# Retention chunks of a hybrid decoder trunk: the cross term is moved beside the scores on TensorE's other row half, and two transposes a chunk take the place of three

## The reference

```python
def retention(q, k, v):
    # chunks of C = 128 tokens; decay, xi, zeta, chunk_decay are fixed numbers of the head
    scores = einsum(qc, kc) * decay
    o_inner = einsum(scores, vc)
    kz = kc * zeta
    def step(R, inp):
        q_n, kz_n, v_n = inp
        o = q_n @ R                       # what earlier chunks add
        R = R * chunk_decay + kz_n.T @ v_n
        return R, o
    o_cross = scan(step, R0, ...) * xi
    return o_inner + o_cross

ro = retention(rope(rq), rope(rk) * 64 ** -0.5, rv)
ra = silu(rg) * group_norm(ro)            # over the 128 columns of a head
mixed = concatenate([ra, dilated_attention], -1)
x = x + mixed @ w_out
```

## Time and profile before

| what | value |
|---|---|
| median of 3 runs | 2365.36 us (2365.22 to 2365.97) |
| the profiled execution | 2364.84 us, of which the traced span is 2363.1 us |
| TensorE busy | 2316.7 us, 98% of the span |
| VectorE, GpSimd, ScalarE busy | 1444.8, 1103.5 and 830.8 us |
| retention heads | four stretches between 100 and 545 us |

### The profile page before, as it was taken

How to read it: one execution, slowest core, us unless ns; L and a number is a source line. 1 busy time by engine, 2 the same in 40 slices (tenths; PEclk the granted TensorE clock), 3 DMA queues, 4 the chain that set the end, 5 groups by cost and what they waited for, 6 DMA issues and landing times.

```text
span 2363.1 us, 34417 instructions
## 1 busy us (share of the span) xinstructions
PE 2316.7 (98%) x12184; PEld 1973.2 (83%) x12184; DVE 1444.8 (61%) x2862; ACT 830.8 (35%) x1701; POOL 1103.5 (47%) x994
## 2 busy tenths in 40 slices
PE   6999999999999999999999999999999999999999
PEld 6888888889978888888887788889978888888887
DVE  6564646462475776577674666662475676577664
ACT  5525243531332233223232555552332233233220
POOL 5323232322174665567464533332184666467461
PEclk9999999999999999999999999999999999999999
DMA  3111111123112111210203111013102210210211
GB/s 128 28 28 28 27 28 28 28 63 94 41 32 72 63 47 32 71 53 18 89 25 114 41 31 30 19 51 103 54 19 72 63 62 18 71 53 23 83 36 72
DMA packets 140981, 120.35 MB, mean 51 GB/s; under 512 B 26048, under 2 KB 126912, under 8 KB 140864
## 3 DMA queue, kind: packets, MB, share of 16 engines
q1 hardware_dynamic: 133488, 103.70, 14.2%
q10 hardware_dynamic: 7376, 15.12, 1.9%
HBM read 110.41 MB, written 8.39 MB: 50 GB/s over the span
## 4 chain that ended last, share of the span: by engine, by line
PE 87%; DVE 7%; POOL 2%; issue 2%; ACT 1%; DMA 1%; SPq 0%; DVEq 0%; ACTq 0%; POOLq 0%
PE gp L483 14%; PE gp L485 13%; PE gp L484 13%; PE sc L485 6%; PE sc L483 6%; PE sc L484 6%; PE o_ps L567 2%; PE tp L484 2%; PE tp L483 2%; PE tp L485 2%; PE sc L546 2%; PE o_ps L603 2%; PE tp L555 1%; PE qt L483 1%; PE qt L485 1%
## 5 line engine op out<-in xcount | busy, mean ns | idle before, releaser
L483 PE MATMUL gp<-W_hi,hT_hi 128*128 128x384 f32 (+1 forms) x1152 | 418.3, 363 | 5.8 <-POOL W_lo L1812 5.5
L485 PE MATMUL gp<-W_hi,hT_lo 128*128 128x384 f32 (+1 forms) x1152 | 381.9, 331 | 0.0
L484 PE MATMUL gp<-W_lo,hT_hi 128*128 128x384 f32 (+1 forms) x1152 | 381.1, 331 | 0.0
L1937 POOL TENSOR_TENSOR W_lo<-af,W_hi 128x512 fp32r<-128x512 f32 x168 | 238.1, 1417 | 282.5 <-ACT W_hi L1094 282.5
L1917 POOL TENSOR_TENSOR W_lo<-raw,W_hi 128x1024 fp32r<-128x1024 f32 x72 | 187.6, 2611 | 230.5 <-ACT W_hi L1036 217.7
L1631 DVE TENSOR_TENSOR af<-af 128x512 f32<-128x512 f32 x112 | 81.2, 725 | 300.5 <-ACT af L1077 300.5
L483 PEld LDWEIGHTS gp<-W_hi,hT_hi 128*128 128x128 f32 x1152 | 218.3, 189 | 40.7 <-issue 31.7
L1937 POOL TENSOR_TENSOR W_lo<-rb,W_hi 128x512 fp32r<-128x512 f32 x168 | 244.2, 1454 | 0.0
L484 PEld LDWEIGHTS gp<-W_lo,hT_hi 128*128 128x128 f32 x1152 | 219.0, 190 | 0.0
L485 PEld LDWEIGHTS gp<-W_hi,hT_lo 128*128 128x128 f32 x1152 | 217.5, 189 | 0.0
L483 PE MATMUL gp<-hT_hi,W_hi 128*128 128x512 f32 x512 | 199.5, 390 | 0.0
(11 more groups left out here) (300 smaller groups left out, 5330.5 us busy)
## 6 DMA issues: line engine op xcount, KB each, us to landing
raw<-in_mlp_w_up SPq DMA_DIRECT2D x64, 512.0 KB, 4.4
rb<-in_mlp_w_down SPq DMA_DIRECT2D x56, 512.0 KB, 5.4
raw<-in_hyb_w_in SPq DMA_DIRECT2D x74, 128.0 KB, 2.4
X<-in_x SPq DMA_DIRECT2D x8, 512.0 KB, 7.5
X<-in_x ACTq DMA_DIRECT2D x8, 512.0 KB, 3.3
raw<-in_mlp_w_down SPq DMA_DIRECT2D x8, 512.0 KB, 3.3
raw<-in_swa_w_qkv SPq DMA_DIRECT2D x16, 256.0 KB, 3.1
x_spill<-X ACTq DMA_DIRECT2D x8, 512.0 KB, 2.6
```

Of the source, the lines that this page charges most:

```text
L483: mm(o, a[0], b[0], start=first, stop=False)
L484: mm(o, a[0], b[1], start=False, stop=False)
L485: return mm(o, a[1], b[0], start=False, stop=last)
L1937: E.tensor_tensor(WF_lo[:, c], x(k), WF_hi[:, c].bitcast(f32), ALU.subtract).then_inc(op_ready, 1)
```

## The change

Four things change. The queries and keys of a chunk now lie next to each other in one tile as k, q, scaled q, scaled k, so two transposes bring k to rows 0 to 63, and q and scaled q to rows 0 to 63 and 64 to 127 of `rqT`. The state R and `r_add` lie on rows 64 to 127. The cross term is issued in `ret_scores`, between the scores and `r_add`, and opens the accumulation in `r_out` that `ret_values` closes. And `ret_scores` takes over the waits for `r_x` and `r_R`. Since the tile `QK` is shared with dilated attention, VectorE and GpSimd get one more wait each at the borders between heads.

```diff
@@ ret_T
-                q, k, qx = rQK[:, r % 2, 0:HD], rQK[:, r % 2, HD:2 * HD], QK[:, r % 2, 4 * HD:5 * HD]
-                for m, src in enumerate((q, k, qx)):
-                    last = nc.tensor.transpose(qt[0:HD, m * P:(m + 1) * P], src, ident[:, :])
-                last.then_inc(r_qt, 1)
+                nc.tensor.transpose(qt[LO, 0:P], QK[:, r % 2, 0:HD], ident[:, :])
+                nc.tensor.transpose(qt[:, P:2 * P], QK[:, r % 2, HD:3 * HD], ident[:, :]).then_inc(r_qt, 1)
@@ ret_scores
                 if r == 0:
                     pe.wait_ge(sm_ready, (g + 1) * U_D)
+                else:
+                    pe.wait_ge(r_x, n)
+                    pe.wait_ge(r_R, n)
                 pe.wait_ge(r_qtev, n + 1)
-                mm(sc[:, 0:P], rqT[:, 1, :], rqT[:, 0, :], start=True, stop=True)
-                mm(r_add, QK[:, r % 2, 5 * HD:6 * HD], v, start=True, stop=True).then_inc(r_st, 1)
+                mm(sc[:, 0:P], rqT[LO, 0, :], rqT[LO, 1, :], start=True, stop=True)
+                if r >= 1:
+                    mm(r_out, rqT[HI, 1, :], rR[HI, r % 2, :], start=True, stop=False)
+                mm(r_add, QK[:, r % 2, 3 * HD:4 * HD], v, start=True, stop=True).then_inc(r_st, 1)
@@ ret_values
                 pe.wait_ge(r_sT, n + 1)
-                if r >= 1:
-                    pe.wait_ge(r_x, n)
-                o = r_out
-                last = mm(o, rsT[:, :], G[:, r % RING, 2 * HD:2 * HD + RV], start=True, stop=(r == 0))
-                if r >= 1:
-                    pe.wait_ge(r_R, n)
-                    last = mm(o, rqT[:, 2, :], rR[:, r % 2, :], start=False, stop=True)
-                last.then_inc(r_o, 1)
+                mm(r_out, rsT[:, :], G[:, r % RING, 2 * HD:2 * HD + RV], start=(r == 0), stop=True).then_inc(r_o, 1)
@@ ret_T_copy (ScalarE)
-                A(rqT[:, :, :].rearrange("p m c -> p (m c)"), qt[0:HD, 0:3 * P], ACT.Copy).then_inc(r_qtev, 1)
+                A(rqT[:, :, :].rearrange("p m c -> p (m c)"), qt[:, 0:2 * P], ACT.Copy).then_inc(r_qtev, 1)
@@ ret_rope (VectorE)
+                if r == 0:
+                    dve.wait_ge(qt_done, n + T)
@@ gains (GpSimd)
                 if t - 1 >= 2:
                     pool.wait_ge(qt_done, a0 + t - 2)
+                elif kind == "D" and a0 > 0:
+                    pool.wait_ge(r_st, a0 - 2 + t)
```

More of the change, by code:

```diff
@@ L162, in hybrid_trunk @@
         rsT = at("rsT", [P, P])
-        rR = at("rR", [HD, 2, RV])
+        rR = at("rR", [P, 2, RV])
         rsg = at("rsg", [P, 2, RV])
         re = at("re", [P, 2, RV])
-        rQK = at("rQK", [P, 2, 2 * HD])
-        rqT = at("rqT", [HD, 3, P])
+        rqT = at("rqT", [P, 2, P])
         off[0] = A0
@@ L216, in hybrid_trunk @@
         half_out = tp[:, 512:1024]
-        r_add = sc[0:HD, P:P + RV]
+        LO, HI = slice(0, HD), slice(HD, 2 * HD)
+        r_add = sc[HI, P:P + RV]
         r_out = sc[:, 512:512 + RV]
@@ L386, in load_R @@
                 v = 2 * RH * HD
-                runs(w_in[0], [(0, HD, h * HD), (HD, HD, RH * HD + h * HD), (2 * HD, RV, v + h * RV),
+                runs(w_in[0], [(0, HD, RH * HD + h * HD), (HD, HD, h * HD), (2 * HD, RV, v + h * RV),
                                (2 * HD + RV, RV, v + RH * RV + h * RV)], first)
@@ L1387, in ret_rope @@
                 step.wait()
-                q = rQK[:, r % 2, :]
-                step.did(E.tensor_tensor(q, rA, rB, ALU.add))
+                k, q, qx, kz = [QK[:, r % 2, m * HD:(m + 1) * HD] for m in range(4)]
+                step.did(E.tensor_tensor(QK[:, r % 2, 0:2 * HD], rA, rB, ALU.add))
                 step.wait()
-                step.did(E.tensor_scalar(QK[:, r % 2, 4 * HD:5 * HD], q[:, 0:HD], xi[:, bass.ds(h, 1)], None, ALU.mult))
-                E.tensor_scalar(QK[:, r % 2, 5 * HD:6 * HD], q[:, HD:2 * HD], zeta[:, bass.ds(h, 1)], None,
-                                ALU.mult).then_inc(r_qk, 1)
+                step.did(E.tensor_scalar(qx, q, xi[:, bass.ds(h, 1)], None, ALU.mult))
+                E.tensor_scalar(kz, k, zeta[:, bass.ds(h, 1)], None, ALU.mult).then_inc(r_qk, 1)
                 dve.wait_ge(r_exp, n + 1)
@@ L1408, in ret_state @@
                                 ALU.mult).then_inc(r_sT, 1)
-                new = rR[:, (r + 1) % 2, :]
+                new = rR[HI, (r + 1) % 2, :]
                 if r == 0:
@@ L1413, in ret_state @@
                     dve.wait_ge(r_R, n)
-                    E.scalar_tensor_tensor(new, rR[:, r % 2, :], cdec[0:HD, bass.ds(h, 1)], r_add,
+                    E.scalar_tensor_tensor(new, rR[HI, r % 2, :], cdec[HI, bass.ds(h, 1)], r_add,
                                            ALU.mult, ALU.add).then_inc(r_R, 1)
```

## The result

| | before | after |
|---|---|---|
| median | 2365.29 us (2362.76 to 2365.97, 4 runs) | 2404.04 us (2401.77 to 2406.45, 4 runs) |
| ratio | | 1.0166, 95% interval 1.0154 to 1.0178 |
| profiled execution, span | 2364.84, 2363.1 us | 2401.95, 2400.2 us |

The kernel got slower by 38.7 us, 1.6%. The direction, the place and the number of the waits were forecast. The size was not: 24 us were forecast, and the time lies 2 us above the range. A second set of 5 runs of the changed kernel gave 2403.95 us against 2365.87, 38.1 more.

A forecast was written before the change was run, and what follows sets the result against it. TensorE was taken as busy nearly throughout, but a loop through VectorE would decide after the change: 11.2 us in three heads plus 13.1 in the last, 24.3 more, 2389.7 us; range 2385 to 2394, with three rivals 2380 to 2402.

The forecast's parts named there:

- TensorE's savings: Retention chunks on TensorE: one transpose fewer, 0.11 us in 32 chunks; cross term off the values, 0.62 in 28; 20.9 us.
- The rival of halves in turn: Scores and cross term on TensorE's row halves run one after the other: 0.41 us more per link, 2399.5 us; chance 0.10.
- The moved wait and its loop: Scores of chunks 2 to 7 wait for the previous result through VectorE: loop 6.75 or 7.91 us, longer in last head.
- VectorE's work keeps its sizes: VectorE's instructions in a retention chunk take as long as before the change; costed at nothing.
- What TensorE no longer does: Prediction's section pricing TensorE work removed or moved in retention: 20.9 us off if TensorE were the bound throughout.
- VectorE's part of the loop: From line 1407 to the end of line 1426 on VectorE: 5.81 us, or 6.97 for chunks 1 to 3.
- The clock: Last head: TensorE's idle waits halve its clock, up to 1.7 us after each of five, so 2398 us; chance 0.10.
- The collision with GpSimd: GpSimd's split of weights makes line 1426 take 1.46 us, not 0.29; stays. Rival, undone: 2376 us, chance 0.11.
- The last head otherwise: Last head's longer loop: 9.98 us between scores, 1.16 more for chunks 2 and 3; 13.1 us added in all.
- Given back later: After the last retention head nothing waits for a fixed time, so none of the loss is recovered.
- The median of runs: Forecast built on the profiled execution, 2364.84 us, giving 2389.2; median taken 0.52 higher, 2389.7 us.

The follow-up runs named there:

- the kernel with the wait alone: Kernel before plus one line: the scores also wait for the previous chunk's r_x, nothing moved; 2400.23 us, ratio 1.0150.
- the one with two outputs: Changed kernel with r_out in another PSUM bank for chunks 3, 5 and 7, scores there waiting for the result two chunks back; 2367.65 us, ratio 1.0013.
- the swapped one: Changed kernel with k and q on rows 64 to 127, and scaled q, state and r_add on rows 0 to 63; 2398.70 us, ratio 1.0151.
- with the clock held: Changed kernel with 14 unused matmuls filling TensorE's idle time ahead of the r_x waits, chunks 3 to 7 of the last head; 2397.49 us, ratio 1.0136.

## Why the prediction was wrong, point by point

- **TensorE's savings: right.** Chunks 0 to 1 of a head are 10.50 us apart instead of 10.63, retention's end gives 0.70 back against 0.62, and the pairing is there. The rival of halves in turn would have cost 0.21 a link and not 0.41.
- **The moved wait and its loop: right.** Place, 24 waits, and the loop's length at the old layout (6.75 and 7.9) are as forecast; the kernel with the wait alone shows them, and the one with two outputs shows that they go with the wait. The waits were forecast at over 2 us where GpSimd's split delays the result: only chunk 3's was (2.6), chunks 2 and 4 waited 1.2 and 1.0.
- **"VectorE's work keeps its sizes": wrong.** This is the step that failed, in the last item of "What TensorE no longer does", where it is costed at nothing; the 5.81 us of VectorE's part of the loop rest on it. The sizes are the same, the start partitions are not: that part measured 6.19, 0.37 us more a chunk, 6.7 us in three heads and 0.6 in the last. By that rule on held instructions the place of this cost, though not its size, could be seen ahead in the diff, as `rR[HI]` and `sc[HI]` follow and precede operands from partition 0.
- **The clock: a rival, with 0.10, and true beside the forecast.** I set it against the forecast though it could only come on top of it. In the last head it cost 2.9 us of the 17.6: 1.43 in each of two distances, where the rival had 1.7 in each of five. In the other heads it cost 0.6 us from chunk 3 to 4 of the third, and some 0.9 behind chunk 7 of the second, where the clock was at 0.50 from 297.8 to 301.3; the other slow stretches there lengthen no distance.
- **The collision with GpSimd: kept, as said.** Line 1423's delays stay in chunks 0 to 3. What I didn't see is a new one, in chunks 6 and 7: 1.3 us in the three heads of the changed kernel, and 0.57 a head in the swapped one.
- **The last head otherwise:** 57.6 + 13.7 = 71.3 us forecast from chunk 0 to chunk 7, 72.4 with the clock held. Of the missing 1.1, some 0.13 in each of five distances goes with the place of the state (chunk 2 to 3 takes 11.25 us, and 11.13 with the halves swapped). The rest is mostly chunk 5 to 6 (10.47, not 9.98); I didn't follow it further.
- **Given back later: not shown.** What follows retention is 1.05 us shorter in this trace. In the second trace of the same kernel it is 1.06 longer than before, so the 1.05 is the spread of single runs, and "it isn't given back" stands.
- **The median of runs.** The forecast of 24.3 and the measured 37.1 are one profiled execution against another. The 1.0 to 1.7 us more between the medians are within the spread of single runs.

Distance by distance, the 37.1 us hold the 24.3 forecast, 7.3 from the place of the state, 4.4 from the clock (2.9, 0.6 and 0.9), 1.3 from the new collision and 0.4 in the last head's chunk 5 to 6, which stays open. That is 0.6 more than 37.1, less than what the stretch behind retention alone differs between two traces of one kernel.

## What to carry to other kernels

Moving a wait from the consumer of the last part to the start of the whole costs nothing only if the event is already past there: compare the end of the event with the start of the instruction that is to wait, chunk by chunk, and look for an engine loop that the new wait closes. If the buffer, and not the data, is what is waited for, a second buffer is the cheap way out; here it alone took the kernel from 1.6% slower to 0.1% slower, and to 0.4% faster together with the halves swapped and its place given to chunk 2 as well. An operand that moves to other partitions keeps its size and still may cost on VectorE: here some 0.12 us at the instruction itself, and as much at each of two later ones that went back.

## What the hardware showed that I had not expected

- VectorE: in this case an instruction behind one with another start partition didn't overlap it. The steps grew from 0.20 to 0.32, from 0.26 to 0.385 and from 0.21 to 0.32 us, the last one with ten instructions between that didn't read PSUM.
- TensorE: two f32 matmuls on different row halves took 0.43 us together, one alone 0.41 to 0.42, and both on the same half 0.64, each up to the start of the matmul behind them.
- TensorE: idle stretches of 3.6 to 3.9 us came with 3.4 to 6.8 us at 1.2 GHz, and in the changed kernel's first trace so did the longest of each earlier head, 2.6 us, while one of 2.7 us in the last head did not. With 2.6 us of filling work and 1.4 us left to wait, two of those in the last head kept 2.4 GHz.
